# Mixture-of-experts stage: a third place for a pair's weights, and results scattered to the tokens' rows

## The reference

```python
g_sel = jnp.argmax(g_logits, axis=-1)
g_w = jnp.take_along_axis(g_prob, g_sel[:, None], axis=1)
e_in = jnp.take_along_axis(e_logits, g_sel[:, None, None], axis=1)[:, 0]
top_v, top_i = lax.top_k(e_in, TOP_K_EXPERTS)            # 2
top_w = jax.nn.softmax(top_v, axis=-1) * g_w
...
a = jnp.einsum('nd,edf->nef', hf, w_gate[g])
b = jnp.einsum('nd,edf->nef', hf, w_up[g])
hid = jax.nn.silu(a) * b * gates[:, g, :, None]
out = out + jnp.einsum('nef,efd->nd', hid, w_down[g])
```

## Time and profile before

| | us |
|---|---|
| median of 3 runs | 1781.07 (1778.80 to 1783.66) |
| the profiled execution, its own time | 1780.79 |
| its span, first to last instruction | 1778.9 |
| experts stage, first turn to last copy | about 1485 to 1749 |
| combine stage and end | about 1755 to 1779 |

### The profile page before, as it was taken

How to read it: one execution, slowest core, us unless ns; L and a number is a source line. 1 busy time by engine, 2 the same in 40 slices (tenths; PEclk the granted TensorE clock), 3 DMA queues, 4 the chain that set the end, 5 groups by cost and what they waited for, 6 DMA issues and landing times. The chain is left out here.

```text
span 1778.9 us, 14121 instructions
## 1 busy us (share of the span) xinstructions
PE 1539.3 (87%) x4914; PEld 731.1 (41%) x4914; DVE 731.3 (41%) x1670; ACT 421.0 (24%) x671; POOL 28.7 (2%) x45
## 2 busy tenths in 40 slices
PE   5999999999999999999958997757978787778882
PEld 2455555555555455444423442323435533222220
DVE  2377767767776500010222883443311423111113
ACT  2334343444442400000010304043112430000000
POOL 0000000000000000000000000000000001000001
PEclk8999999999999999999979998868988898898896
DMA  5121112211011411230300110102204045999995
GB/s 220 48 95 60 48 36 80 74 60 60 24 36 49 165 59 48 71 106 34 133 26 25 49 48 0 54 1 94 107 12 166 17 180 189 418 429 429 428 431 213
DMA packets 37791, 214.41 MB, mean 121 GB/s; under 512 B 4961, under 2 KB 5857, under 8 KB 30690
## 3 DMA queue, kind: packets, MB, share of 16 engines
q1 hardware_dynamic: 33554, 198.42, 29.6%
q0 software_dynamic: 3600, 13.11, 2.0%
q10 hardware_dynamic: 576, 2.10, 0.3%
HBM read 201.03 MB, written 12.58 MB: 120 GB/s over the span
## 5 line engine op out<-in xcount | busy, mean ns | idle before, releaser
L407 PE MATMUL gla_proj<-hT,weight_slots 128*128 128x512 f32 x896 | 394.7, 596 | 7.1 <-PEq L278 7.1
L407 PEld LDWEIGHTS gla_proj<-hT,weight_slots 128*128 128x128 f32 x896 | 168.0, 191 | 203.3 <-issue 203.3
L2199 PE MATMUL ex_p_gu<-weight_slots,ex_rowsT 128*64 128x512 f32 x512 | 137.5, 690 | 44.8 <-DMA weight_slots<-in_w_gu 42.0
L868 PE MATMUL bl_p<-hT,weight_slots 128*128 128x512 f32 x256 | 114.7, 601 | 1.8 <-PEq L158 1.8
L2199 PEld LDWEIGHTS ex_p_gu<-weight_slots,ex_rowsT 128*64 128x64 f32 x512 | 41.2, 155 | 130.8 <-issue 81.4
L2305 DVE TENSOR_TENSOR ex_hidden<-ex_silu,ex_p_gu 128x256 f32<-128x256 f32 x16 | 6.7, 421 | 177.2 <-ACT ex_silu L2260 177.2
L868 PEld LDWEIGHTS bl_p<-hT,weight_slots 128*128 128x128 f32 x256 | 48.8, 192 | 63.0 <-issue 62.5
L561 ACT ACTIVATE gla_level_decay<-gla_level_decay 128x1024 f32<-128x1024 f32 x56 | 59.1, 1057 | 39.3 <-DVE gla_level_decay L690 38.8
L905 ACT ACTIVATE bl_sig<-bl_p 128x512 f32<-128x512 f32 x16 | 9.6, 598 | 215.4 <-PE bl_p L868 215.4
L433 PEld LDWEIGHTS gla_level<-gla_level_q,gla_level_k 128*128 128x128 f32 x448 | 55.0, 192 | 11.5 <-issue 11.5
L2220 PE MATMUL ex_p_Y<-weight_slots,ex_hiddenT 128*64 128x512 f32 x256 | 58.5, 598 | 0.8 <-DVE ex_hiddenT L2309 0.8
(11 more groups left out here) (367 smaller groups left out, 1996.4 us busy)
## 6 DMA issues: line engine op xcount, KB each, us to landing
weight_slots<-in_w_gu SPq DMA_DIRECT2D x32, 2048.0 KB, 16.6
weight_slots<-in_w_dn SPq DMA_DIRECT2D x16, 2048.0 KB, 11.9
weight_slots<-in_w_gla SPq DMA_DIRECT2D x40, 512.0 KB, 3.6
weight_slots<-in_w_merge SPq DMA_DIRECT2D x32, 512.0 KB, 3.8
weight_slots<-in_w_out SPq DMA_DIRECT2D x16, 512.0 KB, 3.3
expert_rows<-ex_y SPq DMA_DIRECT2D x16, 512.0 KB, 12.3
weight_slots<-in_w_v SPq DMA_DIRECT2D x3, 2048.0 KB, 8.0
weight_slots<-in_w_u SPq DMA_DIRECT2D x8, 512.0 KB, 6.3
```

The lines of the kernel that those rows point to most:

```text
L407: last = nc.tensor.matmul(pj[:, n % 2, :], lhsT, rhs, start=(k == 0), stop=(k == KT - 1))
L868: last = nc.tensor.matmul(pp[:, m % 4, :], core.slot(slot)[:, k, :], src[:, k, :], start=(k == 0), stop=(k == KT - 1))
L2199: last = nc.tensor.matmul(pG[rows, e, :], hgT[:, k, rows], gu[e][k // 4][:, x, k % 4, :], start=(k == 0), stop=(k == KT - 1))
```

## The change

- `Core` gets a third place for a pair's weights: gate-up in the memory of `xT` (half 0) and `hT` (half 1), down in a new buffer `weight_slots_3`, which the cross attention uses before for its own tiles. In the routing SP loads pair 2 there: its down once the projection is over, half 0 when the router product is done, half 1 when the rows are stored.
- In the first round pair u stands in place u % 3, and SP loads pair u+3 when pair u is done with its place. The first round is written out on SP and PE (no loop); later rounds keep two places.
- An index now stands for both a token and which of its two experts: `ix_all` holds 2 x token + choice, or 1024 where the slot is empty, `ix_rows` its half, the token or 512. Gathers read `h_rows` with a bound of 511, scatters write `expert_rows` (now 1024 rows) with a bound of 1023. POOL scatters each pair's result straight from `ex_y` and SP stores nothing in the experts stage. DVE clears `ex_rows` once at the start of the routing, so that rows not gathered hold zeros.
- A copy into `ex_y` waits for `y_free`, which POOL raises for the scatter of pair u-1 after it has issued that of pair u.
- The combine loads the two rows of each token as one piece with 4 plain transfers on SP, into `weight_slots_2`. `pos` goes.

The diff, cut to its core:

```diff
+    def place_gu(self, e, h):
+
+        if e == 2:
+            return (self.xT, self.hT)[h][:].rearrange("p k t -> p (k t)").rearrange("p (s c) -> p s c", c=KT * P)
+        return (self.W2, self.W)[e][:, 4 * h:4 * h + 4, :]
+
+    def place_dn(self, e):
+        return self.W3[:] if e == 2 else (self.W2, self.W)[e][:, 8:12, :]
...
+                gu_src2, dn_src2 = core.pair_weights(2)
                 core.load_pair_dn(sp, 1, dn_src)
                 for h in range(2):
                     sp.wait_ge(proj_done, 4 * (h + 1))
                     core.load_pair_gu_half(sp, 1, h, gu_src)
+                core.load_pair_dn(sp, 2, dn_src2)
+                sp.wait_ge(z_done, 1)
+                core.load_pair_gu_half(sp, 2, 0, gu_src2)
+                sp.wait_ge(h_stored, 16 * NB)
+                core.load_pair_gu_half(sp, 2, 1, gu_src2)
...
                 pool.wait_ge(h_stored, 16 * NB)
+                pool.wait_ge(hg_clear, 1)
                 pool.wait_ge(ix_ready, 1)
                 nc.gpsimd.indirect_dma_start(out=hg[:, 0, :], out_offset=None, in_=core.h_rows[:],
-                                             in_offset=bass.IndirectOffsetOnAxis(ap=ix[:, 0:1], axis=0)).then_inc(hg_in[0], 16)
+                                             in_offset=bass.IndirectOffsetOnAxis(ap=ixg[:, 0:1], axis=0),
+                                             bounds_check=T - 1, oob_is_err=False).then_inc(hg_in[0], 16)
...
+                nc.vector.memset(ixg[:, P:P + 3], T)
+                chain(nc.vector.memset(hg[:], 0.0))
+                dve.engine_nop().then_inc(hg_clear, 1)
...
-                nc.vector.tensor_copy(ix[:, 0:PAIRS], pL[:, 0:PAIRS]).then_inc(ix_ready, 1)
+                chain(nc.vector.tensor_scalar(ix[:, 0:PAIRS], pL[:, 0:PAIRS], 2.0 * T, None, ALU.add))
+                nc.vector.tensor_scalar(ixg[:, 0:PAIRS], ix[:, 0:PAIRS], 1, None, ALU.arith_shift_right).then_inc(ix_ready, 1)
...
-                def store(dst, e, value):
-                    sp.wait_ge(ya, value)
-                    sp.wait_ge(yb, value)
-                    sp.dma_start(dst, ys[:, e]).then_inc(y_out[e], 16)
+                def first_round():
+                    for u in range(PAIRS):
+                        if u + 3 < PAIRS:
+                            gu_src, dn_src = core.pair_weights(u + 3)
+                            sp.wait_ge(gu_done, u + 1)
+                            core.load_pair_gu(sp, u % 3, gu_src)
+                            sp.wait_ge(d_done, u + 1)
+                            core.load_pair_dn(sp, u % 3, dn_src)
...
-                run(0)
+
+                first_round()
...
                 def gather(u, e):
-                    col_ = ix[:, u:u + 1] if isinstance(u, int) else ix[:, bass.ds(u, 1)]
                     pool.wait_ge(t_done, u + 1)
-                    chain(nc.gpsimd.tensor_copy(ixc[:, e:e + 1], col_))
+                    chain(nc.gpsimd.tensor_copy(ixc[:, e:e + 1], column(ixg, u)))
                     nc.gpsimd.indirect_dma_start(
                         out=hg[:, e, :], out_offset=None, in_=core.h_rows[:],
-                        in_offset=bass.IndirectOffsetOnAxis(ap=ixc[:, e:e + 1], axis=0)).then_inc(hg_in[e], 16)
+                        in_offset=bass.IndirectOffsetOnAxis(ap=ixc[:, e:e + 1], axis=0),
+                        bounds_check=T - 1, oob_is_err=False).then_inc(hg_in[e], 16)
+
+                def scatter(u, e):
+                    own = ixc[:, 2 + e:3 + e]
+                    chain(nc.gpsimd.tensor_copy(own, column(ix, u)))
+                    pool.wait_ge(ya, u + 2)
+                    nc.gpsimd.tensor_tensor(ixc[:, 4:5], own, own, ALU.add)
+                    pool.wait_ge(yb, u + 2)
+                    nc.gpsimd.tensor_tensor(ixc[:, 5:6], own, own, ALU.add)
+                    nc.gpsimd.indirect_dma_start(
+                        out=core.Y[:], out_offset=bass.IndirectOffsetOnAxis(ap=ixc[:, 2 + e:3 + e], axis=0),
+                        in_=ys[:, e, :], in_offset=None, bounds_check=2 * T - 1, oob_is_err=False).then_inc(y_out[e], 16)
+
+                def y_is_out(e, value):
+                    pool.wait_ge(y_out[e], value)
+                    nc.gpsimd.tensor_tensor(ixc[:, 6:7], ixc[:, 2 + e:3 + e], ixc[:, 2 + e:3 + e], ALU.add).then_inc(y_free, 1)
...
+                    h = r * (n // 2)
+                    gather(first + 3, 1)
+                    scatter(first, 0)
...
+                    with pool.Fori(0, n // 2 - 1) as i:
+                        u = pool.snap(i * 2 + (first + 1))
+                        out = pool.snap(i * 16 + 16 * (h + 1))
+                        gather(u + 3, 0)
+                        scatter(u, 1)
+                        y_is_out(0, out)
+                        gather(u + 4, 1)
+                        scatter(u + 1, 0)
+                        y_is_out(1, out)
...
                 chain = Chain(pool, ix_ready)
+                gather(1, 1)
+                gather(2, 0)
+                chain.restart()
                 run(0)
+                pool.wait_ge(y_out[1], 16 * (PAIRS // 2))
+                for e in range(2):
+                    pool.wait_ge(hg_in[e], 16 * (PAIRS // 2 + 2 - e))
...
+                def first_round():
+                    for u in range(PAIRS):
+                        gate_up(u, u % 2, u % 3, 16 * (u // 3 + 1))
+                        turn(u + 1, (u + 1) % 2, 16 * ((u + 1) // 2 + 1))
+                        if u:
+                            down(u - 1, (u - 1) % 2, (u - 1) % 3, 16 * ((u - 1) // 3 + 1))
+                        turn_hidden(u, u % 2)
+                    u = PAIRS - 1
+                    down(u, u % 2, u % 3, 16 * (u // 3 + 1))
...
-                def copy_y(u, e, w):
+                def copy_y(u, e):
                     act.wait_ge(d_done, u + 1)
-                    act.wait_ge(y_out[e], w)
+                    act.wait_ge(y_free, u + 1)
                     nc.scalar.copy(ys[:, e, 0:512], pY[:, 0, :]).then_inc(ya, 1)
...
-def combine_stage(core, x_rows, gate, pos, most, out):
+def combine_stage(core, x_rows, gate, out):
...
-    with (nc.sbuf_tensor("cb_g", [P, NB, 2, D], F32) as g, nc.Block() as block):
+    rows = core.Y.rearrange("(n p c) d -> n p c d", p=P, c=2)
+    g = core.W2[:, 0:2 * NB, :].rearrange("p (n c) d -> p n c d", c=2)
+    with nc.Block() as block:
...
-        @block.gpsimd
-        def _(pool):
-            def gather(rows):
-                for n in range(NB):
-                    for c in range(2):
-                        nc.gpsimd.indirect_dma_start(
-                            out=g[:, n, c, :], out_offset=None, in_=rows,
-                            in_offset=bass.IndirectOffsetOnAxis(ap=pos[:, c * NB + n:c * NB + n + 1], axis=0))\
-                            .then_inc(got[n], 16)
...
+        @block.sync
+        def _(sp):
+            for n in range(NB):
+                sp.dma_start(g[:, n], rows[n]).then_inc(got[n], 16)
+            for n in range(NB):
+                sp.wait_ge(summed, n + 1)
+                sp.dma_start(out[n * P:(n + 1) * P, :], x_rows[:, n]).then_inc(stored, 16)
+            sp.wait_ge(stored, 16 * NB)
...
-            core.Y = nc.dram_tensor("expert_rows", [P * P, D], F32).ap()
+            core.Y = nc.dram_tensor("expert_rows", [2 * T, D], F32).ap()
             core.W2 = sb("weight_slots_2", [P, SLOTS, KT * P])
+            core.W3 = sb("weight_slots_3", [P, 4, KT * P])
...
-                kmT, vm, omT = sbc("kmT", [P, 4, MEM]), sbc("vm", [P, MEM // P, T]), sbc("omT", [P, 4, T])
+                room3 = core.W3[:].rearrange("p s c -> p (s c)")
+                kmT = room3[:, 0:4 * MEM].rearrange("p (h m) -> p h m", m=MEM)
+                vm = room3[:, 4 * MEM:4 * MEM + 2 * T].rearrange("p (m d) -> p m d", d=T)
+                omT = room3[:, 4 * T:8 * T].rearrange("p (h t) -> p h t", t=T)
```

174 lines of the change are left out of this document (77 added, 97 removed).

## The result

The changed kernel takes **1759.95 us** (median of 4 runs, 1758.28 to 1760.51) against 1781.8 us (1778.8 to 1783.66) for the kernel before: a ratio of 0.9877, 95% interval 0.9862 to 0.9892. The forecast was 1748.5 with a range of 1742 to 1766, so sign and range hold, but the gain is 22 us and not the 32.6 that the terms added up to.

What follows compares the result with a forecast made beforehand. DMA bytes were taken to bound the experts stage. Pair 15's second half at 1702.7 plus d = 4, then 13.8 us to its copied result and the tail, gave span 1746.4 and 1748.5 us; range 1742 to 1766.

Steps and rivals of the forecast that it cites:

- POOL's work and its delayed wait: Experts stage: POOL's gather, scatter, copies, adds and wait for the scatter before cost nothing; 2.8 us of 15.85 a pair.
- rival A: Gathers and scatters: rows past the bound cost as much as real ones, pairs stay 17.07 us, 1765 us; chance 0.12.
- d: Later start of the experts stage's stream, from pair 2's loads in the routing: 4 us, ends 0.3 and 9.5.
- the 1.2 of the last gathers: End of the stream: POOL's last three gathers belong to the empty second round and move nothing, 1.2 us less.
- The clock's step: Start of the experts stage: PE, idle meanwhile, comes back at the lower of its two clocks, 1.7 us more.
- Rival D: POOL's first gather waits for the whole 2 MB load ahead, 4.9 us for 1.5; d 7.4, 1752 us; chance 0.1.
- Gain: one period: Experts stage: loading pair 2 during the routing takes one pair out of the stream and gains one period.
- every pair stands where the one before it stood: Weight stream: each pair takes the previous pair's position; SP's first load in the stage is pair 3's instead of pair 2's.
- A pair's bytes: Experts stage: dropped rows move nothing, 0.26 + 0.26 MB less a pair, 6.82 MB, so 15.85 us instead of 17.07.
- The end: Pair 15's second half to the finish: 13.8 us stay, scatter adds 0.7, combine uses four 1 MB loads, first 4.4 us.
- B: PE's first round as straight code: instruction fetches through full queues cost 1.5 us a pair, about 1771; chance 0.05.
- C: POOL's loop becomes the bound if indirect DMAs are slow: break-even 7.4 us each, about 1859 at 10 us; chance 0.04.

Runs made afterwards that it cites:

- last_half_at_stage: The changed kernel with only the second half of pair 2's gate-up issued at the start of the experts stage instead of in the routing; 1754.93 us.
- two_places: The changed kernel with two weight places: no load of pair 2 in the routing, stream two pairs ahead; 1767.21 us.
- third_alone: The kernel before with only the third place added, filled during the routing; all 128 rows of a pair still gathered and stored; 1773.47 us.
- fill_at_stage: The changed kernel with all three loads of pair 2 issued first thing in the experts stage instead of in the routing; 1756.93 us.
- order_as_pe: The changed kernel with SP issuing loads in the order PE needs them, gate-up of pair u+3 ahead of down of pair u+2; 1752.80 us.
- gather_all: The changed kernel with first-round gather indices limited to row 511, so empty slots fetch a row too; 1765.36 us.
- await_at_once: The changed kernel with POOL waiting for each scatter's end right behind issuing it, before the next gather; 1792.93 us.

## Why the prediction was right, and where its sizes were off

Its main steps hold. The stage is bound by bytes (share 1.01 from 1550 on); PE runs at 12.0 us a pair, ahead of the weights until pair 6, whose first half is the first to wait (1564.01); the bytes per pair are as reckoned (q0 0.53 MB for 0.52); POOL's work and its delayed wait are off the path; from pair 15's second half to its result copied it is 13.8 us as before (1714.21 to 1728.03). But that the time lies in the range is in part luck. The forecast's own range, without rival A, was 1742 to 1757, and 1759.95 is outside it; the range went to 1766 for rival A, which did not happen. The losses all go one way, and none makes up for another. The 10.0 us between the forecast span of 1746.4 and 1756.4 lie in these terms:

| term of the sum | forecast | measured | us |
|---|---|---|---|
| first load of the stream | 1498.7 (d = 4) | 1500.82 | +2.1 |
| from there to pair 6's second half | 1565.25 less 1498.7: 66.55 | 1569.44 less 1500.82: 68.62 | +2.1 |
| pairs 6 to 14 | 8 x 15.85 | 8 x 16.22 | +3.0 |
| pair 14 to 15, with the 1.2 of the last gathers | 14.65 | 14.98 | +0.3 |
| copy to the combine's first load | 7.95 | 9.20 | +1.25 |
| that load to the end | 18.0 | 19.2 | +1.2 |

**The later start, d.** It is larger than the 2.1 us of the table, since in this execution the routing began 1.4 us earlier (its first load at 1418.20, 1419.63 before): from there to the first load of the stream it is 82.62 us against 75.07, so d is 7.55 where the prediction had 4. Its three steps, counted in the same way: the gather goes out 2.3 later (61.21 against 58.90; forecast 1.0 to 1.5). The last store lands as forecast (SP's load that waits for it goes at 60.35, the forecast was 59.9 to 60.4), but the 0.9 us from there to the gather's issue were left out, and the 0.6 taken off for slack was not there, since the barrier follows the landing. The gather lands in 7.3 instead of 5.8, 1.5, as forecast; and the turn (1.94 instead of 1.06) and gate-up 0 (10.04 instead of 7.09) lose 3.8 us at the lower clock, where the prediction had 1.7, from a wait of 2 us. Those are 7.6. The clock's step is the one that was off most, 2.1 us. The prediction took its price from a half gate-up at the lower clock; here all of the turn and more than half of gate-up 0's time ran at it. Why is open: the wait at the barrier, 5.10 us, does not order the runs (above), and the clock stood at 0.50 from 1464 on. last_half_at_stage bears the split out: landing 2.8 less, turn 0.9, gate-up 0 (8.41) 1.6, together the 5.2 by which its first load is earlier.

By the Trainium skill (DMA: Bandwidth & Descriptors, Queues, rings and completion order), an engine finishes one queue's packet, typically 9 to 17 descriptors, before it turns to another. Rival D takes the load for one such packet on each engine, and then the gather would wait for all 4.9 us of it. The trace has 2.8 (7.3 against 4.5 without the load): part of it. So rival D falls as a mechanism, though its number for d, 7.4, is what came out, by other steps.

**Gain: one period.** The prediction credits the filled place with a whole period of 15.85 less d, 11.9 us. The changed kernel less two_places is 7.3, third_alone less before 8.3. The traces give the period, and take off the larger d and 1.4 to 2.2 us for queues that are not full. fill_at_stage shows that d was not the price of the place: the queues are idle at the stage's start anyway, so the time in the routing gives nothing that this time would not, and costs a late start. The shape "every pair stands where the one before it stood" was also too good: SP waits for down u before the gate-up of pair u + 4, and with PE at its 12.0 us a pair this leaves the queues at 382 GB/s until 1550. order_as_pe takes that away (share 1.01 from 1512).

**A pair's bytes.** 0.26 MB less in each direction should give 1.22 us, and gave 0.85. The tiny packets of dropped rows are shown as packets; gather_all puts a moved row over a dropped one at 0.49 us for 64, 0.12 under its bytes, and twice that (gather and scatter) is 0.24 of the 0.37 missing. For the scatter this is carried over, not measured; the last 0.1 us stays open.

**The end.** From the last copy to the combine's first load the scatter was put 0.7 above SP's store, and it is 1.95. The transfer is not the reason. It goes out 0.7 later behind the copy (0.81 against 0.08), but lands in 3.3 us where the store took 4.6, so it is down 4.1 us behind the copy instead of 4.7. From there to the combine's first load it is 5.1 us instead of 2.6, and 2.92 of them are POOL's drain, which starts at 1733.4 when all of POOL's transfers have landed. A drain of 2.9 to 3.0 us stands there in the trace of every version with the scatter; in the kernel before, POOL's drain at this barrier was over long before. What it waits for is open. The combine's last block still waited 1.17 us for its load, where the prediction had all waits gone. The first of the 1 MB loads came at 4.7 us (4.4 forecast).

**The rivals.** A falls by gather_all and the period; B by PE's 12.0 us a pair through the first five pairs of straight code; C by POOL's 1.05 and 1.02 us for an indirect DMA. D is answered under the later start. But C's place was well seen: with the wait one step nearer (await_at_once) POOL is the bound and the kernel slower than before. The prediction's reason for that, a copy that waits some 11 us for its result, was not what happened: POOL's next scatter waits.

## What to carry to other kernels

Before you fill a buffer ahead of a stage, look whether the queues are idle at the stage's start: there the same load cost less here (by 3.0 us for all three parts, 5.0 for the last half), while ahead of the stage it stands in front of the small transfer that the stage's first instruction needs. Issue a ring's loads in the order of use, and free a buffer by halves; in a stage bound by bytes both show only where the queues run dry and at the last byte, but here, with one load moved behind the first gather, they gave 15 us more where the whole change had given 22. Read the drain at the end of a stage as a term of the sum when you move transfers to POOL: 2.9 us here. An engine that issues indirect DMAs and waits for them in its own order is a loop of its own: add up landing and issue, and keep the sum a whole step below the period.

## What the runs showed of the hardware

- At the barrier that ends the routing POOL's drain lasts until the indirect DMA that POOL has issued has landed: 7.64 and 6.08 us with the gather ahead of it, 34 ns without. That is not all a drain can hold: at the end of the experts stage it took 2.92 us after every transfer of POOL had landed.
- A row dropped by the bound leaves a packet: 2083 packets under 512 bytes in 150 us, against 1400 with the gather's drops gone and 698 in the kernel before. A gather of which half is dropped still lands in a median of 14.3 us beside full queues.
- Of two indirect DMAs that POOL issues 2 us apart beside busy queues, the second takes some 4 us longer from issue to landing: gather 14.3 and scatter 10.2 with the scatter first (share 1.01), 11.1 and 15.3 with the gather first (share 0.91).
- Stores of 512 KB from ACT's queue, 2.6 us each with the queues empty, take 11.4 us beside three 2 MB loads, of which some 2 us came through to the gather behind them; the list of indices covered the rest.
- PE kept at a granted clock of 1.00 through the routing was at 0.50 again a few us into the experts stage, behind a wait of 4.91 us at the barrier in one run and of 0.56 us in another.
